# Layer-norm sums by additions of halves instead of strided reductions, and the last down-projection slab of two feed-forward blocks multiplied in three fp32r parts instead of whole in fp32

## The chip, the cores and the metric

One core of one Trainium2 chip runs the whole program. The metric is the device time of one execution in microseconds (us). Its engines are TensorE (PE, with its weight loads shown apart as PEld), VectorE (DVE), ScalarE (ACT), GpSimd (POOL) and SyncE (SP), which issues the transfers.

## The reference, cut to what matters

Two transformer-like blocks on 256 tokens of width 1024, everything in float32. The part at hand stands in the second block's convolution module and in the feed-forward network (FFN) beside it:

```
def layernorm(x, g, b):
    mu = mean(x, axis=-1)
    var = mean(square(x - mu), axis=-1)
    return (x - mu) * rsqrt(var + EPS) * g + b

def conformer_conv(h, ...):
    u = h @ w_pw1 + b_pw1
    a, g = split(u, 2)
    v = dwconv(a * sigmoid(g), w_dw, b_dw)      # 31 taps
    v = silu(layernorm(v, ln_g, ln_b))
    return v @ w_pw2 + b_pw2

def conv_ffn(h, w_up, w_dw, b_dw, w_down):      # hidden width 2816 = 22 tiles of 128
    u = dwconv(h @ w_up, w_dw, b_dw)            # 3 taps
    a, b = split(u, 2)
    return (silu(a) * b) @ w_down
```

The convolution module runs twice (on the context, then on the latent tokens). The FFN runs four times.

## The kernel before

**Slabs.** Activations lie transposed: 128 features per partition, 256 tokens in the free dimension, 8 tiles for the width 1024. All weights come in slabs of 128 x 2048 floats (1 MB) through a ring of three buffers (`raw`, `whi`, `wlo`). SP loads a slab into `raw`. A *split* slab is then cut in two fp32r parts: ACT writes the upper part (`hi`, L895, `whi`), DVE the rest (`lo`, L1396, `wlo`, columns 0 to 1983), and POOL the last 64 columns of the rest (L853). PE multiplies it by `mm3` (L2052 to L2054), three fp32r matmuls for each product: upper by upper, upper by the activation's lower part, lower by upper. A *whole* slab is not cut: PE takes `raw` in plain fp32 (L703). `kept_whole` says which is which, `DOWN_SPLIT` which down slabs of the FFNs `ffn0` and `ffn_ctx` are split.

**The FFN.** It has 11 steps j = 0 to 10 (`NJ` = 11), each with two up slabs and one down slab. I number the 33 slabs of one FFN from 0. Step 8 has the up slabs 23 and 24 and the down slab 28, step 9 has 26, 27 and 31, step 10 has 29, 30 and 32 (the last one, `use + "_end"`). Slabs 33 to 36 are those of the projection after the convolution (`pw2`). PE's order at the end is: up 26, 27, down 28, up 29, 30, down 31, down 32, then `pw2` slab 33, a mean over squares (`means`, L2153), 34, and so on. For each step ACT writes the first tap from PSUM (`tap`, L504), DVE adds the other taps (`taps`, L592, half 0 into `cva`, half 1 into `cvb`), ACT applies SiLU (L528), DVE multiplies (L617, this is the FFN's middle activation). For a split down slab ACT and DVE then also cut this activation in `m_hi` (L540) and `m_lo` (L626); for a whole one PE reads `cvb` as it is.

**The hosted convolution.** `ffn0` and `ffn_ctx` each carry the convolution module of one copy as "host" work: between the FFN's own instructions, at fixed (j, place) points, DVE and ACT do the 31 taps, and at the end the layer norm: at step 8 `ln_sum` (sum of the 8 tiles of `acc`), PE's `ln_mean`, `ln_centre` (L1579); at step 9 ACT's squares, `ln_fold` (sums of the squares), PE's `ln_var`, ACT's root, `ln_scale` (L1583, L1587); at step 10 ACT's `ln_silu` in two halves of four tiles (L979, with the copies L975 into `h_hi` or `g_hi`), DVE's `ln_lo` (L1592). PE's means multiply the partial sums by a matrix of 1/1024 (L2146), which adds over partitions. The output of this norm is what `pw2` multiplies.

**What sets the order.** Each engine runs its own written-out list; semaphores join them, and an instruction that waits holds everything behind it on its engine. On ACT the call of `hi` for slab 32 stands at the start of step 10, the ones for slabs 33 and 34 behind all of step 10; on DVE `lo` for slab 33 stands behind `ln_lo`. `hi` waits for the slab's transfer and for PE to be done with the slab that last used the same `whi` buffer (three slabs back). Behind the FFN, DVE adds the result to the residual (L1800 for `ffn0`, L1617 for `ffn_ctx`), ACT squares it, DVE folds the squares (L1404, L1406) and PE's `means` uses them behind slab 33.

Of the kernel before, what the change touches and what calls it, by code (L numbers as in the profile page):

```python
# [21 lines left out]
ALU = mybir.AluOpType  # L22
AX = mybir.AxisListType

P = 128
T = 256
# [13 lines left out]
NJ = D_FF // SLABC  # L40
FT = D_FF // P
TAPS = 3
CONV_TAPS = 31
DOWN_SPLIT = (NJ - 3, NJ - 2)
ADD_SLOTS = [(0, 1), (0, 2)] + [(1, at) for at in range(3)] + [(j, at) for j in range(2, NJ - 3) for at in range(3)]
OWN_SLOTS = [j for j in range(2, NJ - 3)]
PRODUCTS = len(ADD_SLOTS)
# [139 lines left out]
def kept_whole():  # L187

    out = []
    for use, i in KEYS:  # L190
        ffn = use.removesuffix("_end")
        if use == "lead":
            out.append(STREAM[i][0] == "ada")
        elif use.startswith("ada"):
            out.append(True)
        elif ffn in DOWN_WHOLE:
            out.append(use != ffn or (i >= 4 and i % 3 == 1 and (i - 4) // 3 not in DOWN_SPLIT))
        else:
            out.append(False)
    return out  # L200
# [75 lines left out]
def build(nc, io):  # L276
# [10 lines left out]
    with ctx:  # L287
# [7 lines left out]
        ps = ctx.enter_context(nc.psum_tensor("ps", [P, 8, 512], F32))  # L295
# [17 lines left out]
        bufA = sb("bufA", [P, SLAB])  # L313
# [8 lines left out]
        ones = sb("ones", [P, P])  # L322
# [12 lines left out]
        def flat(a):  # L335
            names = "abc"[:len(a.shape) - 1]
            return a.rearrange(f"p {' '.join(names)} -> p ({' '.join(names)})")
# [12 lines left out]
        acc = sra  # L350
# [7 lines left out]
        lstd = g_flat[:, late + 2 * T + 3 * P:late + 4 * T + 3 * P].rearrange("p (a t) -> p a t", a=2)  # L358
# [3 lines left out]
        ctx_sq, ctx_y = flat(mqk[:, :, :, :]), flat(sra[:, :, :])  # L362
# [40 lines left out]
        dve_order, act_order, pool_order = sem("dve_order"), sem("act_order"), sem("pool_order")  # L403
# [25 lines left out]
        sg_done, v_done, pads_done, dw_done = sem("sigmoid_done"), sem("glu_done"), sem("pads_cleared"), sem("dwconv_folded")  # L429
        mu_done, cen_done, lsq_done, var_done = sem("ln_mean_done"), sem("ln_centred"), sem("ln_squared"), sem("ln_var_done")  # L430
        lfold_done = sem("ln_folded")
# [955 lines left out]
        def _(dve):  # L1387
            order = Tally(dve_order)
# [174 lines left out]
            def ln_sum(q):  # L1563

                dve.wait_ge(prod_used, PRODUCTS * (q + 1))
                dve.wait_ge(dve_order, order.value())
                if q:
                    dve.wait_ge(lnorm_done, 2 * q)
                dve.tensor_reduce(lstd[:, 0, :], acc[:, :, :].rearrange("p t n -> p n t"), AX.X, ALU.add).then_inc(dw_done, 1)

            def ln_fold(q):
                for i in range(2):
                    dve.wait_ge(lsq_done, 2 * q + i + 1)
                    dve.tensor_reduce(lstd[:, i, :], ctx_sq[:, 1024 * i:1024 * i + 1024].rearrange("p (t n) -> p n t", n=T),  # L1574
                                      AX.X, ALU.add).then_inc(lfold_done, 1)

            def ln_centre(q):
                dve.wait_ge(mu_done, q + 1)
# [470 lines left out]
        def _(pe):  # L2049
# [92 lines left out]
            def mean(sums, bank, done, ready, first):  # L2142

                for i, s in enumerate(sums):
                    pe.wait_ge(ready, first + i + 1)
                    ins = pe.matmul(ps[:, bank, 0:T], ones[:, :], s, start=(i == 0), stop=(i == len(sums) - 1))  # L2146
                ins.then_inc(done, 1)
# [8 lines left out]
            def means_of_pairs(n, sq, k0, k1, bank=4):  # L2156
# [6 lines left out]
                if k1 == 4:  # L2163
                    ins.then_inc(ms_done, 1)

            def ln_mean(q):
                mean([lstd[:, 0, :]], 0, mu_done, dw_done, q)

            def ln_var(q):
                mean([lstd[:, 0, :], lstd[:, 1, :]], 1, var_done, lfold_done, 2 * q)  # L2170

            def conv_pe(q):

# [650 lines left out]
```

## Time and profile before

| what | us |
|---|---|
| median of 3 runs (lowest to highest) | 1391.59 (1390.79 to 1392.91) |
| the profiled execution's own time | 1392.44 |
| its span in the trace | 1390.7 |
| PE busy in the span | 1365.9 |
| DVE busy | 988.7 |
| ACT busy | 839.6 |
| POOL busy | 401.9 |

The trace covers the span of the profiled execution; 1.7 us of its time lie around it. Busy is the time in which at least one instruction of an engine runs; a matmul that waits for the one in front of it counts as busy. PE is busy almost throughout, so what matters is where PE stops, and how long its own instructions take.

### The profile page before, as it was taken

How to read it: one execution, taken by the hardware profiler on the slowest of the kernel's cores; microseconds unless marked ns; L12 is line 12 of the kernel's file. 1: busy time of each engine (PE TensorE's matmuls, PEld its weight loads, DVE VectorE, ACT ScalarE, POOL GpSimd, SP SyncE). 2: the span in 40 equal slices, each digit the busy share in tenths (PEclk: the TensorE clock that was granted, in tenths of full speed). 3: DMA queues.
4: the chain of work that ended last, by engine and by line, in shares of the span. 5: the costliest groups of instructions: out<-in, count | busy, mean ns of one | idle time of the engine just before them, and what ended most of it. 6: DMA issues, size and time to landing. Idle time of an engine off the chain costs nothing.

```text
span 1390.7 us, 26228 instructions
## 1 busy us (share of the span) xinstructions
PE 1365.9 (98%) x10670; PEld 1269.9 (91%) x10670; DVE 988.7 (71%) x1292; ACT 839.6 (60%) x1214; POOL 401.9 (29%) x194
## 2 busy tenths in 40 slices
PE   7999999999999999999999999999999999999997
PEld 4888889999999999999999999999998868999996
DVE  3322684868799998878999989766667696654446
ACT  3532555647888856567888575555544486644554
POOL 1452434233110011241100101656652201233332
PEclk9999999999999999999999999999999999999999
DMA  8776765455343454674434547655554713455551
GB/s 315 267 262 244 266 233 214 158 197 192 147 182 158 156 200 177 263 268 160 158 160 180 214 148 273 219 212 214 214 185 180 271 45 127 182 182 181 181 185 57
DMA packets 39576, 272.07 MB, mean 196 GB/s; under 512 B 4612, under 2 KB 5892, under 8 KB 6974
## 3 DMA queue, kind: packets, MB, share of 16 engines
q1 hardware_dynamic: 39486, 270.81, 52.7%
q8 instruction: 64, 1.05, 0.3%
q14 instruction: 26, 0.21, 0.0%
HBM read 269.73 MB, written 1.06 MB: 195 GB/s over the span
## 4 chain that ended last, share of the span: by engine, by line
PE 89%; DVE 7%; ACT 2%; DMA 1%; issue 1%; SPq 0%; DVEq 0%; ACTq 0%
PE ps L2052 23%; PE ps L2053 22%; PE ps L2054 22%; PE ps L703 9%; PE ps L2198 3%; PE ps L2089 2%; DVE wlo L1396 2%; DMA raw<-w_dram 1%; PE ps L2099 1%; PE ps L2566 1%; PE ps L2552 1%; DVE gates L1574 1%; ACT whi L895 1%; PE ps L2501 1%; PE ps L2248 1%
## 5 line engine op out<-in xcount | busy, mean ns | idle before, releaser
L853 POOL TENSOR_TENSOR wlo<-raw,whi 128x64 fp32r<-128x64 f32 (+1 forms) x185 | 399.6, 2162 | 968.5 <-ACT whi L895 968.3
L895 ACT ACTIVATE whi<-raw 128x2048 fp32r<-128x2048 f32 x185 | 352.8, 1911 | 358.9 <-PE ps L2054 223.1
L1396 DVE TENSOR_TENSOR wlo<-raw,whi 128x1984 fp32r<-128x1984 f32 (+1 forms) x185 | 338.7, 1832 | 309.2 <-ACT whi L895 309.2
L2052 PE MATMUL ps<-h_hi,whi 128*128 128x256 f32 x1232 | 354.1, 287 | 0.0
L2053 PE MATMUL ps<-h_lo,whi 128*128 128x256 f32 x1232 | 348.4, 283 | 0.0
L2054 PE MATMUL ps<-h_hi,wlo 128*128 128x256 f32 x1232 | 348.4, 283 | 0.0
L2052 PE MATMUL ps<-g_hi,whi 128*128 128x256 f32 x1040 | 298.4, 287 | 0.0
L2053 PE MATMUL ps<-g_lo,whi 128*128 128x256 f32 x1040 | 294.2, 283 | 0.0
L2054 PE MATMUL ps<-g_hi,wlo 128*128 128x256 f32 x1040 | 294.1, 283 | 0.0
L2052 PEld LDWEIGHTS ps<-h_hi,whi 128*128 128x128 f32 x1232 | 236.0, 192 | 8.0 <-issue 6.8
L2053 PEld LDWEIGHTS ps<-h_lo,whi 128*128 128x128 f32 x1232 | 236.1, 192 | 0.8
L2054 PEld LDWEIGHTS ps<-h_hi,wlo 128*128 128x128 f32 x1232 | 236.1, 192 | 0.0
L2052 PEld LDWEIGHTS ps<-g_hi,whi 128*128 128x128 f32 x1040 | 199.4, 192 | 3.7 <-issue 2.9
L2053 PEld LDWEIGHTS ps<-g_lo,whi 128*128 128x128 f32 x1040 | 199.4, 192 | 0.4
L2054 PEld LDWEIGHTS ps<-g_hi,wlo 128*128 128x128 f32 x1040 | 199.4, 192 | 0.0
L703 PE MATMUL ps<-cvb,raw 128*128 128x256 f32 x576 | 127.4, 379 | 0.5 <-DVE cvb L617 0.5
L703 PEld LDWEIGHTS ps<-cvb,raw 128*128 128x128 f32 x576 | 108.2, 190 | 14.9 <-issue 0.9
L995 ACT ACTIVATE bufA<-gates,cols 128x256 f32<-128x256 f32 x192 | 79.5, 502 | 23.4 <-DVE sra L1523 23.4
L592 DVE SCALAR_TENSOR_TENSOR cvb<-ps,cols,cvb 128x255 f32<-128x255 f32 (+1 forms) x176 | 76.5, 476 | 9.9 <-ACT cvb L504 6.6
L995 ACT ACTIVATE bufB<-gates,cols 128x256 f32<-128x256 f32 x176 | 72.8, 502 | 17.5 <-DVE sra L1523 17.5
L592 DVE SCALAR_TENSOR_TENSOR cva<-ps,cols,cva 128x255 f32<-128x255 f32 (+1 forms) x176 | 76.5, 475 | 3.3 <-DVE cva L592 0.3
L2052 PE MATMUL ps<-m_hi,whi 128*128 128x256 f32 x272 | 77.0, 283 | 0.0
(318 smaller groups left out, 1936.2 us busy)
## 6 DMA issues: line engine op xcount, KB each, us to landing
raw<-w_dram SPq DMA_DIRECT2D x243, 1024.0 KB, 4.9
sra<-w_dram SPq DMA_DIRECT2D x2, 1024.0 KB, 6.0
mqk<-w_dram SPq DMA_DIRECT2D x2, 1024.0 KB, 5.8
brev<-w_dram SPq DMA_DIRECT2D x2, 1024.0 KB, 7.6
gates<-w_dram SPq DMA_DIRECT2D x2, 1024.0 KB, 8.5
xlat<-xT_dram SPq DMA_DIRECT2D x2, 512.0 KB, 4.5
brev<-w_first_keys_dram SPq DMA_DIRECT2D x1, 1024.0 KB, 9.3
brev<-bias_rows SPq DMA_DIRECT2D x1, 1024.0 KB, 8.7
```

What stands on the lines that cost most here:

```text
L592: ins = dve.scalar_tensor_tensor(out, ps[:, 2 * par + half, m * T + src:m * T + src + n], w, out, ALU.mult, ALU.add)
L703: ins = pe.matmul(ps[:, 4 + m // 2, (m % 2) * T:(m % 2) * T + T], wf[:, k, m * P:m * P + P], cvb[:, par, k, :], start=(first and k == 0 an ...
L853: pool.tensor_tensor(wlo[:, g.slot, part], raw[:, g.slot, part], whi[:, g.slot, part].bitcast(F32), ALU.subtract).then_inc(lo2_done, 1)
L895: act.activation(whi[:, g.slot, :], raw[:, g.slot, :], ACT.Copy).then_inc(hi_done, 1)
L995: ins = act.activation(buf[:, t * T:t * T + T], vpad[:, t, k:k + T], ACT.Copy, scale=col("dw_w", KT * k + t))
L1396: dve.tensor_tensor(wlo[:, g.slot, part], raw[:, g.slot, part], whi[:, g.slot, part].bitcast(F32), ALU.subtract)\
L1574: dve.tensor_reduce(lstd[:, i, :], ctx_sq[:, 1024 * i:1024 * i + 1024].rearrange("p (t n) -> p n t", n=T), AX.X, ALU.add).then_inc(lfold_d ...
L2052: pe.matmul(out, w[0], x[0], start=start, stop=False, skip_group_check=True)
L2053: pe.matmul(out, w[0], x[1], start=False, stop=False, skip_group_check=True)
L2054: return pe.matmul(out, w[1], x[0], start=False, stop=stop, skip_group_check=True)
L2089: pe.matmul(ps[:, bank, m * T:m * T + T], w[i][:, k, m * P:m * P + P], x[0][:, k, :], start=(k == 0 and m == 0 and i == 0), stop=False, sk ...
L2198: ins = pe.matmul(ps[r:r + QUAD, bank, 0:SLABC], cnd[:, c:c + QUAD], w[:, t, :], start=(t < 4 and k == 0), stop=(t >= 4 and k == n - 1), s ...
```

## The change

It does three things. `ln_sum` and `ln_fold` no longer use a reduction over strided elements, but add halves in place: 8 tiles to 4 to 2 (into `bufA`) for the sum, and 4 to 2 twice and then 2 + 2 for the squares. The last addition over the remaining two tiles is left to PE, in `total`, which waits once and multiplies two tiles: `ln_mean` has two matmuls where it had one, `ln_var` two as before. The wait of the second `ln_sum` on the norm before it is gone. And `DOWN_SPLIT` has step 10 too, so that slab 32 of `ffn0` and of `ffn_ctx` is split, with its `m_hi` and `m_lo`.

```
-DOWN_SPLIT = (NJ - 3, NJ - 2)
+DOWN_SPLIT = (NJ - 3, NJ - 2, NJ - 1)
...
-            out.append(use != ffn or (i >= 4 and i % 3 == 1 and (i - 4) // 3 not in DOWN_SPLIT))
+            out.append(NJ - 1 not in DOWN_SPLIT if use != ffn else i >= 4 and i % 3 == 1 and (i - 4) // 3 not in DOWN_SPLIT)
...
                 dve.wait_ge(prod_used, PRODUCTS * (q + 1))
                 dve.wait_ge(dve_order, order.value())
-                if q:
-                    dve.wait_ge(lnorm_done, 2 * q)
-                dve.tensor_reduce(lstd[:, 0, :], acc[:, :, :].rearrange("p t n -> p n t"), AX.X, ALU.add).then_inc(dw_done, 1)
+                order.mark(dve.tensor_tensor(bufA[:, 0:4 * T], flat(acc[:, 0:4, :]), flat(acc[:, 4:8, :]), ALU.add))
+                dve.wait_ge(dve_order, order.value())
+                dve.tensor_tensor(bufA[:, 0:2 * T], bufA[:, 0:2 * T], bufA[:, 2 * T:4 * T], ALU.add).then_inc(dw_done, 1)

             def ln_fold(q):
                 for i in range(2):
                     dve.wait_ge(lsq_done, 2 * q + i + 1)
-                    dve.tensor_reduce(lstd[:, i, :], ctx_sq[:, 1024 * i:1024 * i + 1024].rearrange("p (t n) -> p n t", n=T),
-                                      AX.X, ALU.add).then_inc(lfold_done, 1)
+                    half = ctx_sq[:, 1024 * i:1024 * i + 512]
+                    order.mark(dve.tensor_tensor(half, half, ctx_sq[:, 1024 * i + 512:1024 * i + 1024], ALU.add))
+                dve.wait_ge(dve_order, order.value())
+                dve.tensor_tensor(ctx_sq[:, 0:512], ctx_sq[:, 0:512], ctx_sq[:, 1024:1536], ALU.add).then_inc(lfold_done, 1)
...
+            def total(rows, bank, done, ready, n):
+
+                pe.wait_ge(ready, n + 1)
+                for i, row in enumerate(rows):
+                    ins = pe.matmul(ps[:, bank, 0:T], ones[:, :], row, start=(i == 0), stop=(i == len(rows) - 1))
+                ins.then_inc(done, 1)
+
             def ln_mean(q):
-                mean([lstd[:, 0, :]], 0, mu_done, dw_done, q)
+                total([bufA[:, T * i:T * i + T] for i in range(2)], 0, mu_done, dw_done, q)

             def ln_var(q):
-                mean([lstd[:, 0, :], lstd[:, 1, :]], 1, var_done, lfold_done, 2 * q)
+                total([ctx_sq[:, T * i:T * i + T] for i in range(2)], 1, var_done, lfold_done, q)
```

On VectorE, in step 10 of `ffn0`, this stood before (the middle line L1587 is `ln_scale`, L592 the taps, L617 the middle activation, L1592 `ln_lo`, L1396 the `lo` of slab 33):

```order
L1587 TENSOR_TENSOR sra<-sra,gates 128x1024
L592 SCALAR_TENSOR_TENSOR cva<-ps,cols,cva 128x254 [waits tap0_done]
L592 SCALAR_TENSOR_TENSOR cva<-ps,cols,cva 128x254
L592 SCALAR_TENSOR_TENSOR cva<-ps,cols,cva 128x255 [waits dve_order]
L592 SCALAR_TENSOR_TENSOR cva<-ps,cols,cva 128x255
L592 SCALAR_TENSOR_TENSOR cvb<-ps,cols,cvb 128x254 [waits tap0_done]
L592 SCALAR_TENSOR_TENSOR cvb<-ps,cols,cvb 128x254
L592 SCALAR_TENSOR_TENSOR cvb<-ps,cols,cvb 128x255 [waits dve_order]
L592 SCALAR_TENSOR_TENSOR cvb<-ps,cols,cvb 128x255
L617 TENSOR_TENSOR cvb<-cva,cvb 128x512 [waits conv_done,silu_done]
L1592 TENSOR_TENSOR h_lo<-mqk,h_hi 128x512 [waits conv_act_hi_done] x4
L1396 TENSOR_TENSOR wlo<-raw,whi 128x1984 [waits slab_hi_done]
```

In the changed kernel the same place on VectorE begins and ends like this (line numbers behind the edits are 2 higher, so L1589 is the old L1587 and L1594 the old L1592):

```order
L1589 TENSOR_TENSOR sra<-sra,gates 128x1024
L1396 TENSOR_TENSOR wlo<-raw,whi 128x1984 [waits slab_hi_done]
L592 SCALAR_TENSOR_TENSOR cva<-ps,cols,cva 128x254 [waits tap0_done]
...
L617 TENSOR_TENSOR cvb<-cva,cvb 128x512 [waits conv_done,silu_done]
L626 TENSOR_TENSOR m_lo<-cvb,m_hi 128x512 [waits host_mid_hi_done]
L1594 TENSOR_TENSOR h_lo<-mqk,h_hi 128x512 [waits conv_act_hi_done] x4
L1396 TENSOR_TENSOR wlo<-raw,whi 128x1984 [waits slab_hi_done]
```

So `lo` of slab 32 now stands ahead of the taps of step 10, and `m_lo` ahead of `ln_lo`.

On ScalarE, at the end of step 10 of `ffn0`, this stood before (L528 is the SiLU of step 10, L979 and L975 are the second half of `ln_silu`, L895 the `hi` of slabs 33 and 34):

```order
L528 ACTIVATE cva<-cva 128x512 [waits conv_done]
L979 ACTIVATE mqk<-sra,cols 128x256 [waits ln_normed] x2
L975 ACTIVATE h_hi<-mqk 128x512 [waits ln_silu_done]
L979 ACTIVATE mqk<-sra,cols 128x256 [waits ln_normed] x2
L975 ACTIVATE h_hi<-mqk 128x512 [waits ln_silu_done] x2
L895 ACTIVATE whi<-raw 128x2048 [waits slab_used,slab_landed1]
L895 ACTIVATE whi<-raw 128x2048 [waits slab_used,slab_landed2]
```

In the changed kernel ScalarE has there:

```order
L528 ACTIVATE cva<-cva 128x512 [waits conv_done]
L540 ACTIVATE m_hi<-cvb 128x512 [waits slab_used,mid_done]
L979 ACTIVATE mqk<-sra,cols 128x256 [waits ln_normed] x2
L975 ACTIVATE h_hi<-mqk 128x512 [waits ln_silu_done]
L979 ACTIVATE mqk<-sra,cols 128x256 [waits ln_normed] x2
L975 ACTIVATE h_hi<-mqk 128x512 [waits ln_silu_done] x2
L895 ACTIVATE whi<-raw 128x2048 [waits slab_used,slab_landed1]
L895 ACTIVATE whi<-raw 128x2048 [waits slab_used,slab_landed2]
```

The added `m_hi` waits for the middle activation of step 10 (`mid_done`), and the second half of `ln_silu` and both `hi` stand behind it. A further `hi`, that of slab 32, now stands at the start of step 10.

## Rows read from the trace of the kernel before

**Rows 1.** Page: busy time (share) of TensorE; chain that ended last, by engine.

```profile
PE 1365.9 (98%) x10670; PEld 1269.9 (91%) x10670; DVE 988.7 (71%) x1292; ACT 839.6 (60%) x1214; POOL 401.9 (29%) x194
PE 89%; DVE 7%; ACT 2%; DMA 1%; issue 1%; SPq 0%; DVEq 0%; ACTq 0%
```

**Rows 2.** Windows, TensorE: stretch, its length, PE busy, clock, DMA share, GB/s.

```profile
493.02:499.93 6.91, 6.91 (x35) 1.00 0.01 2
499.93:505.68 5.75, 5.75 (x50) 1.00 0.78 293
536.33:543.48 7.15, 7.15 (x34) 1.00 0.00 0
```

**Rows 3.** Timeline of TensorE (start, us, instruction [idle before]): the means.

```profile
505.68 0.59 PE L2146 MATMUL ps<-gates,ones 128*128 128x256 f32 x2
...
506.22 0.28 PE L2053 MATMUL ps<-g_lo,whi 128*128 128x256 f32 x1
...
549.06 1.02 PE L2153 MATMUL ps<-bufB,ones 128*128 128x256 f32 x4
```

**Rows 4.** Waits, 500 to 552: waiter, releaser, us, times, longest.

```profile
PEld ps L703 <- issue: 0.4, 1, 0.4
PEld ps L2146 <- DVE gates L1574: 0.3, 1, 0.3
```

**Rows 5.** Timeline of VectorE, 500 to 552, end of `ffn0`.

```profile
500.31 3.84 DVE L1569 TENSOR_REDUCE gates<-sra 128x256 f32<-128x2048 f32 x1
...
506.91 2.23 DVE L1396 TENSOR_TENSOR wlo<-raw,whi 128x1984 fp32r<-128x1984 f32 x1 [0.28 <-ACT whi L895]
509.05 0.81 DVE L626 TENSOR_TENSOR m_lo<-cvb,m_hi 128x512 fp32r<-128x512 f32 x1
...
514.12 3.93 DVE L1574 TENSOR_REDUCE gates<-mqk 128x256 f32<-128x1024 f32 x2
...
524.28 2.22 DVE L1396 TENSOR_TENSOR wlo<-raw,whi 128x1984 fp32r<-128x1984 f32 x1
...
528.80 2.36 DVE L1587 TENSOR_TENSOR sra<-sra,gates 128x1024 f32<-128x1024 f32 x2
531.08 1.77 DVE L592 SCALAR_TENSOR_TENSOR cva<-ps,cols,cva 128x254 f32<-128x254 f32 x4
533.60 1.78 DVE L592 SCALAR_TENSOR_TENSOR cvb<-ps,cols,cvb 128x254 f32<-128x254 f32 x4 [0.75 <-ACT cvb L504]
535.49 0.69 DVE L617 TENSOR_TENSOR cvb<-cva,cvb 128x512 f32<-128x512 f32 x1
...
539.45 2.23 DVE L1396 TENSOR_TENSOR wlo<-raw,whi 128x1984 fp32r<-128x1984 f32 x1 [0.86 <-ACT whi L895]
...
546.25 1.29 DVE L1404 TENSOR_TENSOR bufB<-bufB 128x512 f32<-128x512 f32 x2
547.57 0.69 DVE L1406 TENSOR_TENSOR bufB<-bufB 128x512 f32<-128x512 f32 x1
```

**Rows 6.** Timeline of ScalarE, the same stretch.

```profile
504.96 1.92 ACT L895 ACTIVATE whi<-raw 128x2048 fp32r<-128x2048 f32 x1 [6.04 <-DMA raw<-w_dram]
...
521.17 1.90 ACT L895 ACTIVATE whi<-raw 128x2048 fp32r<-128x2048 f32 x1
524.40 0.64 ACT L540 ACTIVATE m_hi<-cvb 128x512 fp32r<-128x512 f32 x1 [1.32 <-DVE cvb L617]
...
533.99 1.08 ACT L979 ACTIVATE mqk<-sra,cols 128x256 f32<-128x256 f32 x2
...
537.52 3.70 ACT L895 ACTIVATE whi<-raw 128x2048 fp32r<-128x2048 f32 x2
```

**Rows 7.** Timeline of GpSimd: its share of a slab.

```profile
550.19 2.37 POOL L853 TENSOR_TENSOR wlo<-raw,whi 128x64 fp32r<-128x64 f32 x1 [8.05 <-ACT whi L895]
```

**Rows 8.** Timeline of VectorE behind `ffn_ctx`, the second copy.

```profile
823.27 2.22 DVE L1396 TENSOR_TENSOR wlo<-raw,whi 128x1984 fp32r<-128x1984 f32 x1 [0.86 <-ACT whi L895]
...
832.00 0.69 DVE L1406 TENSOR_TENSOR bufB<-bufB 128x512 f32<-128x512 f32 x1
```

## The prediction

> **What bounds the kernel now.** I read the page first: TensorE is busy 98% of the span and the chain that ended last runs through it for 89% [rows 1]. So only two things move the time: a shorter or longer list of TensorE's own instructions, and stops of TensorE. Next the waits of the stretch in which the change lies (500 to 552 us for `ffn0`, the same picture 823.27 - 539.45 = 283.8 us later for `ffn_ctx` [rows 5, 8]): TensorE stops twice, 0.3 us before `ln_var`'s second matmul, which waits for the reduction L1574, and 0.4 us before the whole slab 32 (L703), whose middle activation (L617, 535.49 + 0.69 = 536.18) is just late [rows 4, 5]. The reader should see from this that TensorE comes to slab 32 at 535.9, and that VectorE and ScalarE are only just in time there: behind 514 VectorE has almost no idle time in its rows [rows 5]. What is added to these two engines there is not hidden.
>
> **What TensorE's own list gains.** In a dense stretch a whole down slab (32 records) takes 6.91 us, a slab of 48 fp32r matmuls 5.75 [rows 2], so splitting slab 32 saves 1.16 us. From its start to the next slab it took 7.15 [rows 2], 0.24 more than dense; in the new form I take 5.75 + 0.1 = 5.85. `ln_mean` gets a second fp32 matmul. One costs 0.42: behind it the second fp32r matmul starts at 506.22, where without it it would start at 505.68 + 0.12 (the pitch, 5.75 / 48) [rows 2, 3]. The 0.3 us wait in `ln_var` goes, but part of it lay over the matmuls' own time, so I count 0.15 of it. Net TensorE reaches slab 32 at 535.9 - 0.15 + 0.42, so 0.3 later, at 536.15.
>
> **What the additions of halves gain on VectorE.** `ln_sum` falls from 3.84 to one addition of 1024 elements (2.36 / 2 = 1.18, L1587) and one of 512 (0.69): 1.9 saved [rows 5]. `ln_fold` falls from 3.93 to 1.29 + 0.69 (L1404 and L1406 do just this): again 1.9 saved [rows 5]. But where does the time go?
> - The first 1.9 go nowhere. Soon behind `ln_sum` VectorE waits for ScalarE's `hi` of slab 28 (the 0.28 idle before 506.91), and that starts at 504.96 because of its transfer [rows 5, 6]. The wait becomes 2.2 us and everything behind it stands as before. TensorE did not wait for `ln_sum` either.
> - Of the second 1.9, half arrives. The `lo` of slab 31 (524.28) could start at 522.4, but its `hi` runs from 521.17 to 523.07 [rows 5, 6], and that, behind the root and the SiLU, hangs on `ln_var`, which comes about 0.2 later. So 523.35: 0.95 saved. `ln_scale` ends at 530.15 and not 531.08.
>
> **What the split of slab 32 costs.** Step by step in `ffn0`:
> - VectorE's `lo` of slab 32 stands ahead of the taps. 524.28 + 2.22 overlaps its follower by 0.1, so 2.13 [rows 5]. Taps of half 0 start at 530.15 + 2.15 = 532.3 instead of 531.08. Half 1 before waited 0.75 for ScalarE (533.60); that cover takes up part: it starts at 534.05, 0.45 later. The middle activation is written at 536.6, not 536.18 [rows 5].
> - ScalarE's `m_hi` waits for it and takes 0.64 [rows 6], VectorE's `m_lo` 0.81 [rows 5]: slab 32 may start at 536.6 + 0.65 + 0.8 + two hand-overs of 0.06 = 538.15. TensorE, there at 536.15, waits 2.0 us, and ends at 538.15 + 5.85 = 544.0. Before it was 543.48. So the split's own saving is already more than gone: +0.5.
> - Behind `m_hi` on ScalarE are queued the second half of `ln_silu` and then the `hi` of slab 33. Before, they started right behind the SiLU, at 533.99 and 537.52 [rows 6]: 3.53 us for the half. Now the half starts at 537.2, so `hi` of slab 33 at 540.75, and VectorE's `lo` at 542.7, not 539.45 [rows 5]: +3.25. GpSimd's 64 columns of the same slab take 2.37 beside it [rows 7], against VectorE's 2.2, and TensorE needs both. So `pw2` starts at 542.7 + 2.4 + 0.05 = 545.15. Before it was 543.48, and TensorE waits another 1.15: +1.7.
> - VectorE next adds the residual, cuts slab 34 and folds the squares. From `lo` of slab 33 to the end of L1406 that is 547.57 + 0.69 - 539.45 = 8.81 us [rows 5], so the fold is ready at 551.5. TensorE is through slab 33 at 545.15 + 5.75 = 550.9 and waits 0.7. Its `means` start at 551.6, before at 549.06 [rows 3]: +2.5. That margin was under 1 us, so it is what is late next. Behind it the same chains hang on TensorE's own progress and shift with it; I give nothing back.
>
> `ffn_ctx` is the same but for its residual: 832.00 + 0.69 - 823.27 = 9.42 from `lo` to fold [rows 8], 0.6 longer, and so +3.1. Sum: 2.5 + 3.1 = **+5.6 us**. The `lo` of slab 32 also lets SP load slab 35 some 11 us earlier than TensorE's end of slab 32 did; nothing on TensorE waited for it, so I count zero, and if another load were late it would be a gain, not a loss.
>
> The trace is of an execution of 1392.44, with a span of 1390.7; it is 0.85 above the median of 1391.59. The sum is a difference of the span, so I put it on the median: 1391.6 + 5.5, **1397.1 us**.
>
> **A rule weighed.** The row gives 3.84 us for the reduction of 2048 elements and 1.9 for the two additions in its place [rows 5]. The Trainium skill ("VectorE: DVE Perf Modes", Rules for kernel authors) says that `tensor_reduce` is the slowest VectorE operation and that one on a hot path is worth restructuring. The rows agree on the price, but not that this path is hot: by the rule 7.6 us of VectorE's time in the two copies would come off the end, by the rows at most 0.95 in each reaches slab 32, and without the split the additions alone would be worth 0.1 to 0.3 us a copy.
>
> **Bounds of what the trace doesn't show.** `total` with its one wait: zero to 0.4 a copy. A split slab 32 behind a wait: 5.75 to 6.1. `m_hi` plus `m_lo` with the hand-overs: 1.4 (the nearest rows without hand-over) to 1.9. Residual and fold under a busy GpSimd: plus 0 to 0.4. Together -1.0 to +2.0 on the sum for both copies.
>
> **The rivals.**
> 1. *All of VectorE's saving arrives* (no change, chance 0.08). Then slab 32's parts are ready 2.8 earlier, at 535.35; TensorE does not wait and ends at 542.0, but `m_hi` still pushes the `hi` of slab 33: its `lo` starts at 539.9, `pw2` at 542.35 (-1.1), the fold is ready at 548.75 (-0.3), in `ffn_ctx` +0.3. Sum about 0: 1391.6. Against it: the transfer behind the 6.04 us idle on ScalarE [rows 6].
> 2. *Only TensorE's list counts* (faster, 0.05). The order behind `m_hi` costs nothing, slab 32 starts at 536.15 and ends at 542.0, and slab 33's `lo` and the fold are ready in time: -1.45 a copy, -2.9: 1388.7. It decides itself where `lo` of slab 33 ends by 542 and the fold by 547.8; before they ended at 541.7 and 548.26 [rows 5], so it needs that ScalarE's queue is not moved at all. The list says that it is.
> 3. *Slab 32 waits, but nothing behind it does* (no change, 0.06): +0.5 a copy, 1392.6. It needs `lo` of slab 33 by 543.8, while I have 544.9.
> 4. *A further stop behind `means`* (slower, 0.06). The next fold, for `means` before `pw2` slab 36, is also just in time; if TensorE waits there 1 us a copy more, 1399 to 1401.
> My forecast as worked out has 0.75.
>
> **How the numbers follow.** A difference of 0.2% (2.8 us) is about what a measurement of this kernel can tell from none. The forecast's own range is 1396 to 1399. For 8 in 10 the range takes in rival 3 and the near half of rival 4: 1392.6 to 1399.6; rivals 1 and 2 stay outside. Slower by over 0.2%: the forecast and rival 4, 0.81; within: rivals 1 and 3, 0.14; faster 0.05.
>
> **What the new profile would show.** Right if: VectorE's idle before the `lo` of slab 28 is 2.2 us; TensorE waits for `m_lo` some 2 us before slab 32, then about 1 us for L1396 or L853 before `pw2`, then 0.7 to 1.3 us before `means`; `hi` of slab 33 starts 3.2 us later against slab 32's activation. Wrong if: the `lo` of slab 31 follows without ScalarE's `hi` (rival 1), or if `pw2` follows slab 32 without a gap (rivals 2 and 3), or if the copies differ by much more than 0.6 us.

## The result and the profile after

The changed kernel takes 1398.61 us (median of 5 runs, 1395.18 to 1401.67), the kernel before in the same session 1390.79 (5 runs, 1389.42 to 1392.91). The ratio is 1.0053 with a 95% interval of 1.0038 to 1.0068: by this ratio it is slower by 7.4 us, interval 5.3 to 9.5 (the two medians differ by 7.8). A second session, with the changed kernel unchanged (told below), gave 1.0032 (1.0017 to 1.0048), or 4.4 us (medians 5.2 apart). The two intervals overlap. The prediction was +5.6 and 1397.1, in the range of 1392.6 to 1399.6.

The page of the changed kernel, busy time and the chain that ended last, beside [rows 1]:

```profile
span 1399.7 us, 26320 instructions
...
PE 1366.3 (98%) x10706; PEld 1271.8 (91%) x10706; DVE 983.5 (70%) x1300; ACT 843.7 (60%) x1218; POOL 407.9 (29%) x196
...
PE 88%; DVE 6%; ACT 2%; DMA 2%; issue 1%; SPq 0%; POOL 0%; DVEq 0%; ACTq 0%
```

VectorE has 5.2 us less work, TensorE 0.4 more, and the span is 9.0 longer. So the time is in stops of TensorE. Its weight loads show them (PEld: start, duration, what is loaded, idle before). Those with an idle time, in `ffn0` and then in `ffn_ctx`:

```profile
540.80 0.19 PEld L2054 LDWEIGHTS ps<-m_hi,whi 128*128 128x128 f32 x1 [2.07 <-issue]
547.96 0.19 PEld L2054 LDWEIGHTS ps<-h_hi,whi 128*128 128x128 f32 x1 [1.34 <-issue]
554.07 0.73 PEld L2155 LDWEIGHTS ps<-bufB,ones 128*128 128x128 f32 x4 [0.30 <-DVE bufB L1406]
...
827.11 0.19 PEld L2054 LDWEIGHTS ps<-m_hi,whi 128*128 128x128 f32 x1 [2.07 <-issue]
834.27 0.19 PEld L2054 LDWEIGHTS ps<-g_hi,whi 128*128 128x128 f32 x1 [1.34 <-issue]
841.12 0.73 PEld L2155 LDWEIGHTS ps<-bufB,ones 128*128 128x128 f32 x4 [1.05 <-DVE bufB L1406]
```

These are the stops before slab 32, before `pw2` slab 33 and before `means`, where before there were only 0.3 in `ln_var` and 0.4 ahead of slab 32 [rows 4]. The waits of TensorE's instructions from 500 to 560 name who is late:

```profile
PE ps L2054 <- DVE m_lo L626: 1.9, 1, 1.9
...
PE ps L2054 <- POOL wlo L853: 1.2, 1, 1.2
...
PEld ps L2155 <- DVE bufB L1406: 0.3, 1, 0.3
```

VectorE in the same stretch, beside [rows 5]. This execution came to the stretch 2.61 later than that of before (first weight load of slab 25 at 495.52 and at 492.91), so 2.61 is to be taken off a start before it is compared:

```profile
502.97 1.22 DVE L1567 TENSOR_TENSOR bufA<-sra 128x1024 f32<-128x1024 f32 x1
504.22 0.69 DVE L1569 TENSOR_TENSOR bufA<-bufA 128x512 f32<-128x512 f32 x1
...
509.55 2.23 DVE L1396 TENSOR_TENSOR wlo<-raw,whi 128x1984 fp32r<-128x1984 f32 x1 [2.14 <-ACT whi L895]
...
525.97 2.23 DVE L1396 TENSOR_TENSOR wlo<-raw,whi 128x1984 fp32r<-128x1984 f32 x1 [0.89 <-ACT whi L895]
...
530.62 2.36 DVE L1589 TENSOR_TENSOR sra<-sra,gates 128x1024 f32<-128x1024 f32 x2
532.90 2.22 DVE L1396 TENSOR_TENSOR wlo<-raw,whi 128x1984 fp32r<-128x1984 f32 x1
...
538.61 0.69 DVE L617 TENSOR_TENSOR cvb<-cva,cvb 128x512 f32<-128x512 f32 x1
540.00 0.69 DVE L626 TENSOR_TENSOR m_lo<-cvb,m_hi 128x512 fp32r<-128x512 f32 x1 [0.69 <-ACT m_hi L540]
...
545.33 2.22 DVE L1396 TENSOR_TENSOR wlo<-raw,whi 128x1984 fp32r<-128x1984 f32 x1 [1.03 <-ACT whi L895]
...
553.32 0.69 DVE L1406 TENSOR_TENSOR bufB<-bufB 128x512 f32<-128x512 f32 x1
```

The additions save what they should. All that `ln_sum` saves turns into idle time before the `lo` of slab 28 (2.14, before 0.28). Of what `ln_fold` saves about half does, before the `lo` of slab 31 (0.89, before none), and the other half arrives: that `lo` starts at 525.97 - 2.61 = 523.36, before at 524.28 [rows 5]. ScalarE shows the queue behind `m_hi`, beside [rows 6]:

```profile
539.33 0.63 ACT L540 ACTIVATE m_hi<-cvb 128x512 fp32r<-128x512 f32 x1 [1.85 <-DVE cvb L617]
539.87 1.08 ACT L979 ACTIVATE mqk<-sra,cols 128x256 f32<-128x256 f32 x2
...
543.40 3.70 ACT L895 ACTIVATE whi<-raw 128x2048 fp32r<-128x2048 f32 x2
```

The `hi` of slab 33 starts at 543.40 - 2.61 = 540.79, before at 537.52 [rows 6]: 3.27 later.

To compare kernels without what lies outside, I use **the stretch**: from the first weight load of slab 25 to the weight load of the `means` behind `pw2` slab 33. Before it is 548.95 - 492.91 = 56.04 in `ffn0` and 56.07 in `ffn_ctx`; after, 554.07 - 495.52 = 58.55 and 841.12 - 781.82 = 59.30. So +2.51 and +3.23, together +5.74. The span differs by 9.0. The rest is 2.61 ahead of the stretch, where no code of the change has run yet, and 0.65 behind the second copy. The 2.61 are not the change's: the same changed kernel in the second session came to the stretch at 491.48, which is 4.04 earlier and also ahead of the kernel before.

### The profile page after: what moved, and what is told of

Its sections match the earlier page's. It is cut to its first block, busy times and chain, and to the rows that moved or that the text cites. A ratio compares the mean times of both kernels' runs of the same rounds, so it can differ in the third digit from the quotient of the medians.

```text
span 1399.7 us, 26320 instructions
## 1 busy us (share of the span) xinstructions
PE 1366.3 (98%) x10706; PEld 1271.8 (91%) x10706; DVE 983.5 (70%) x1300; ACT 843.7 (60%) x1218; POOL 407.9 (29%) x196
## 3 DMA queue, kind: packets, MB, share of 16 engines
q8 instruction: 64, 1.05, 0.3%
## 4 chain that ended last, share of the span: by engine, by line
PE 88%; DVE 6%; ACT 2%; DMA 2%; issue 1%; SPq 0%; POOL 0%; DVEq 0%; ACTq 0%
PE ps L2054 23%; PE ps L2055 22%; PE ps L2056 22%; PE ps L703 8%; PE ps L2207 3%; PE ps L2091 2%; DMA raw<-w_dram 2%; DVE wlo L1396 2%; PE ps L2101 1%; PE ps L2575 1%; ACT whi L895 1%; PE ps L2561 1%; PE ps L2510 1%; PE ps L2257 1%; DVE tiny L1902 0%
## 5 line engine op out<-in xcount | busy, mean ns | idle before, releaser
L853 POOL TENSOR_TENSOR wlo<-raw,whi 128x64 fp32r<-128x64 f32 (+1 forms) x187 | 405.7, 2171 | 971.5 <-ACT whi L895 971.2
L895 ACT ACTIVATE whi<-raw 128x2048 fp32r<-128x2048 f32 x187 | 356.5, 1910 | 361.7 <-PE ps L2056 228.5
L1396 DVE TENSOR_TENSOR wlo<-raw,whi 128x1984 fp32r<-128x1984 f32 (+1 forms) x187 | 339.3, 1816 | 320.5 <-ACT whi L895 320.4
L703 PE MATMUL ps<-cvb,raw 128*128 128x256 f32 x512 | 113.2, 379 | 0.0
L703 PEld LDWEIGHTS ps<-cvb,raw 128*128 128x128 f32 x512 | 96.2, 190 | 12.4
L2054 PE MATMUL ps<-m_hi,whi 128*128 128x256 f32 x304 | 86.2, 283 | 3.8 <-DVE m_lo L626 3.8
L2055 PE MATMUL ps<-m_lo,whi 128*128 128x256 f32 x304 | 86.0, 283 | 0.0
L2056 PE MATMUL ps<-m_hi,wlo 128*128 128x256 f32 x304 | 86.0, 283 | 0.0
```

The source lines that it names most:

```text
L703: ins = pe.matmul(ps[:, 4 + m // 2, (m % 2) * T:(m % 2) * T + T], wf[:, k, m * P:m * P + P], cvb[:, par, k, :], start=(first and k == 0 an ...
L853: pool.tensor_tensor(wlo[:, g.slot, part], raw[:, g.slot, part], whi[:, g.slot, part].bitcast(F32), ALU.subtract).then_inc(lo2_done, 1)
L895: act.activation(whi[:, g.slot, :], raw[:, g.slot, :], ACT.Copy).then_inc(hi_done, 1)
L1396: dve.tensor_tensor(wlo[:, g.slot, part], raw[:, g.slot, part], whi[:, g.slot, part].bitcast(F32), ALU.subtract)\
L2054: pe.matmul(out, w[0], x[0], start=start, stop=False, skip_group_check=True)
L2055: pe.matmul(out, w[0], x[1], start=False, stop=False, skip_group_check=True)
```

## The experiments

The stretch of each run (copy 1, copy 2), TensorE's stop before slab 32 in it, and the measured time. Where there is one run, no ratio is given; there the stretch and the stops are the evidence. Each ratio is to runs of the kernel before in the same session; its medians there were 1390.79, then 1390.00, 1390.20 and 1390.22.

| kernel | stretch | stop before slab 32 | median us (runs) | ratio to before, 95% |
|---|---|---|---|---|
| before | 56.04, 56.07 | 0.43 | | |
| after | 58.55, 59.30 | 2.07 | 1398.61 (5) | 1.0053, 1.0038 to 1.0068 |
| after, repeated | 58.56, 59.31 | 2.07 | 1395.36 (10) | 1.0032, 1.0017 to 1.0048 |
| additions only | 55.80, 55.80 | none | 1388.79 (11) | 0.9988, 0.998 to 0.9997 |
| split only | 59.44, 60.12 | 3.10 | 1398.62 (6) | 1.0056, 1.0042 to 1.007 |
| `hi` of slab 33 early | 58.27, 56.97 | 2.06 | 1393.28 (9) | 1.0024, 1.0014 to 1.0034 |
| GpSimd, slabs 31 and 32 | 59.05, 59.81 | 2.57 | 1396.49 (1) | |
| GpSimd, slab 32 | 58.70, 59.44 | 2.22 | 1398.88 (1) | |
| all three moves | 58.67, 58.79 | 2.71 | 1395.70 (10) | 1.0044, 1.0028 to 1.006 |
| two moves, no GpSimd | 56.27, 56.46 | 1.56 | 1389.95 (12) | 1.0002, 0.9988 to 1.0015 |
| additions, one matmul | 54.94, 54.95 | none | 1387.51 (12) | 0.9977, 0.9964 to 0.999 |
| `ln_sum` only | 56.03, 55.93 | 0.42 | 1392.99 (1) | |
| `ln_fold` only | 54.94, 54.94 | none | 1386.34 (1) | |

The load of `ln_mean` stands 12.65 behind the first load of slab 25 in every kernel (to 0.01), so the stretch can be counted from either.

**The change taken apart.** My theory: the loss is all the split's, through the two queues (VectorE ahead of the middle activation, ScalarE behind `m_hi`), and the additions gain a little. The rival: the additions or the second matmul cost something too. First the additions alone, so the changed kernel with

```
-DOWN_SPLIT = (NJ - 3, NJ - 2, NJ - 1)
+DOWN_SPLIT = (NJ - 3, NJ - 2)
```

> The additions of halves and `total` without the split of slab 32. The stretch is that from TensorE's first weight load of slab 25 to that of the `means` behind `pw2` slab 33: 56.04 us (first copy) and 56.07 (second) before, 58.55 and 59.30 after the change. Queue theory (the split's work on VectorE and ScalarE costs the time): 55.9 in both copies, since slab 32 is whole again and ready before TensorE comes to it (its wait of 0.4 goes), while `ln_mean` has a matmul of 0.42 more and `ln_var` loses its 0.3 wait; whole kernel -0.3 us, ratio 0.998 to 1.001. VectorE's idle before the `lo` of slab 28 is still 2.1 us. Rival (the additions themselves or the changed waits cost the time): the stretch stays at 57.5 or more.

Measured: a stretch of 55.80 in both copies, where before it was 56.04, and 0.9988. TensorE stops nowhere in it. The additions cost nothing; they gain 0.24 in the first copy and 0.27 in the second. The rival falls as a reason for the loss; the second matmul does cost its 0.43, as the kernel with one matmul shows below.

Then the split alone: the kernel before with its strided reductions, and only `DOWN_SPLIT` and the rule in `kept_whole` as in the change.

> The split of slab 32 with the old strided reductions. Queue theory: VectorE comes to the `lo` of slab 32 some 0.95 us later than in the changed kernel, so TensorE waits 3.2 us before slab 32, 1.2 before `pw2`, 0.7 and 1.3 before `means`: the stretch is 59.4 and 60.0 us, the whole kernel +7.3 us, ratio 1.004 to 1.007. Rival (VectorE's lateness isn't what holds slab 32, but ScalarE's `hi` of slab 32 is): the stretch is that of the changed kernel, 58.55 and 59.30.

Measured: 59.44 and 60.12. TensorE's weight loads with an idle time, in this kernel:

```profile
537.75 0.19 PEld L2052 LDWEIGHTS ps<-m_hi,whi 128*128 128x128 f32 x1 [3.10 <-issue]
551.02 0.73 PEld L2153 LDWEIGHTS ps<-bufB,ones 128*128 128x128 f32 x4 [0.20 <-DVE bufB L1406]
```

The stop before slab 32 is 3.10 and not 2.07. Counted from the start of the stretch, slab 32 starts at 46.17 here and at 45.28 in the changed kernel: these 0.89 are what reaches it of the additions in `ln_fold`. The expected stop of 1.2 before `pw2` is gone, because slab 32 itself took 7.23 here and not 5.82, at a lower TensorE clock (below). So the split alone costs 3.40 and 4.05 in the copies, and the additions give 0.9 and 0.8 of it back.

**The queue behind `m_hi`.** If the stops before `pw2` and `means` come from what is queued behind `m_hi`, they go when the `hi` of slab 33 is issued ahead of it. In the changed kernel, ScalarE and then VectorE:

```
                 tap(1, j, par)
+                if ends and whole:
+                    hi(g + (RING + 1))
...
-            for k in range(ahead):
+            for k in range(1 if whole else 0, ahead):
                 hi(g + (RING + 1 + k))
...
                        .then_inc(hostmid_lo, host_step(j))
+                    if ends:
+                        lo(g + (RING + 1))
...
-            lo(g + (RING + 1))
+            if not whole:
+                lo(g + (RING + 1))
```

> The changed kernel with only two calls moved: ScalarE's `hi` of slab 33 stands behind the tap of half 1 of step 10, where ScalarE idles 1.5 us, and VectorE's `lo` of slab 33 right behind `m_lo` of step 10. Queue theory: the 2 us wait before slab 32 stays (2.0 to 2.5), the waits before `pw2` (1.3) and `means` (0.3 and 1.05) go; the stretch is 56.7 and 57.0 us, the whole kernel +1.5 us against before, ratio 1.000 to 1.003. Rival (the waits before `pw2` come from slab 32's late end itself, not from the order behind `m_hi`): the stretch stays above 58.

Measured: one stop in each copy, before slab 32, 2.06 and 2.07; none before `pw2` or `means`. Copy 2 has 56.97, as expected, copy 1 58.27. The windows of this kernel say why (length, PE busy and number of instructions, PEld, DVE, ACT, POOL, then the granted clock, DMA share and GB/s):

```profile
536.60:540.00 3.40, 3.40 (x18) 3.40 (x17) 3.40 (x6) 3.40 (x5) 0.00 (x0) 0.50 0.38 99
...
822.60:826.00 3.40, 3.40 (x30) 3.40 (x30) 3.40 (x6) 3.40 (x5) 0.00 (x0) 1.00 0.43 92
```

In copy 1 the granted clock was 0.50 (1.2 GHz and not 2.4) for 3.4 us in the middle of slab 32: 18 matmuls recorded where copy 2 has 30. That is what sets the copies apart: slab 32 took 7.23 in copy 1 and 5.74 in copy 2. The queue is confirmed as the cause of the two later stops: 59.30 - 56.97 = 2.3 us in copy 2. The two calls were moved together, so which of the two queues holds more of it is not shown.

**GpSimd takes half of the rest.** To shorten VectorE's queue ahead of the middle activation I gave GpSimd 1024 of the 2048 columns of `lo` in place of 64, for slabs 31 and 32:

```
+    if use in DOWN_WHOLE and i == 3 * NJ - 2 or use in ("ffn0_end", "ffn_ctx_end"):
+        return 1024
```

> The changed kernel with GpSimd taking 1024 of the 2048 columns of slabs 31 and 32 instead of 64, so that VectorE's two `lo` take 1.36 and not 2.22 us each. Queue theory (VectorE's work ahead of slab 32 sets its start): everything behind comes 1.7 us earlier, TensorE waits 0.4 before slab 32 and not 2.0; the stretch is 56.9 and 57.6 us. Rival (ScalarE's `m_hi` or GpSimd is what is late): the wait before slab 32 stays at 1.5 or more, since GpSimd's 3.4 us for 1024 columns end later than VectorE's.

Measured: the stop before slab 32 is 2.57, longer than without. A miss. GpSimd and VectorE of this kernel show it:

```profile
519.94 6.26 POOL L855 TENSOR_TENSOR wlo<-raw,whi 128x1024 fp32r<-128x1024 f32 x2 [7.10 <-ACT whi L897]
```

```profile
519.90 1.23 DVE L1398 TENSOR_TENSOR wlo<-raw,whi 128x1024 fp32r<-128x1024 f32 x1 [0.93 <-ACT whi L897]
521.04 2.90 DVE L628 TENSOR_TENSOR m_lo<-cvb,m_hi 128x512 fp32r<-128x512 f32 x1
523.87 1.74 DVE L1587 RECIPROCAL gates<-gates 128x256 f32<-128x256 f32 x1
525.64 2.78 DVE L1591 TENSOR_TENSOR sra<-sra,gates 128x1024 f32<-128x1024 f32 x2
528.35 1.21 DVE L1398 TENSOR_TENSOR wlo<-raw,whi 128x1024 fp32r<-128x1024 f32 x1
529.49 1.77 DVE L594 SCALAR_TENSOR_TENSOR cva<-ps,cols,cva 128x254 f32<-128x254 f32 x4
```

The `lo` itself fell from 2.22 to 1.2, but `m_lo` took 2.90 where it took 0.81, and the two multiplications of `ln_scale` 2.78 where they took 2.36. That is 2.5 lost for 2.0 saved, and the stop grew by 0.5. The first of GpSimd's two instructions ends at 523.40, while `m_lo`, begun at 521.04, ends at 523.94. To see whether slab 31's share was the trouble, the same for slab 32 alone:

```
+    if use in ("ffn0_end", "ffn_ctx_end"):
+        return 1024
```

> The changed kernel with GpSimd taking 1024 columns of slab 32 alone, no longer of slab 31. Contention theory (in e4_pool_share VectorE's `m_lo` of step 9 and the `ln_scale` took 2.9 and 2.8 us beside GpSimd's 1024 columns of slab 31, instead of 0.8 and 2.4, which ate the saving): here GpSimd's run lies beside the taps; if these read their second input from PSUM they are not slowed, TensorE waits 1.1 us before slab 32 and not 2.07, and the stretch is 57.6 and 58.3. Rival (any VectorE work beside a long GpSimd run is slowed): the wait is 2 us or more, and the taps of step 10 take over 2 us and not 1.77.

Measured: 2.22, a miss again. GpSimd and VectorE:

```profile
525.87 2.40 POOL L855 TENSOR_TENSOR wlo<-raw,whi 128x1024 fp32r<-128x1024 f32 x1 [1.14 <-ACT whi L897]
```

```profile
526.98 3.51 DVE L1591 TENSOR_TENSOR sra<-sra,gates 128x1024 f32<-128x1024 f32 x2
530.42 1.21 DVE L1398 TENSOR_TENSOR wlo<-raw,whi 128x1024 fp32r<-128x1024 f32 x1
531.55 1.77 DVE L594 SCALAR_TENSOR_TENSOR cva<-ps,cols,cva 128x254 f32<-128x254 f32 x4
```

Now `ln_scale` runs 3.51: 1.15 more than its 2.36. GpSimd's instruction ends at 525.87 + 2.40 = 528.27, 1.29 behind `ln_scale`'s start. So the first multiplication seems to stand until GpSimd is through, and what `lo` saves (1.0) is paid just ahead of it. The Trainium skill says this ("SBUF — State Buffer", SBUF: two separate sides, and Who interferes with whom): GpSimd and a VectorE instruction with two SBUF inputs share one pair of ports, whoever starts first holds it for the whole instruction, and with at most one SBUF input, outside its two-port modes, VectorE is free of it. The rows agree in size: 528.27 plus two multiplications of 1.18 is 530.63, and `ln_scale` ended at 530.49. They agree in kind too: L1587, the reciprocal, has one SBUF input, ran beside GpSimd in the kernel with both shares (at 523.87) and took its usual 1.74.

**All moves together.** The early `hi` of slab 33, GpSimd's 1024 columns of slab 32, and the second half of `ln_scale` moved behind the middle activation of step 10:

```
                 if hosting:
                     beside(1)
+                if whole and ends:
+                    beside(1.5)
...
+                    if (j, at) == (NJ - 1, 1.5):
+                        ln_scale_half(KT // 2)
```

> The changed kernel with three moves: `hi` and `lo` of slab 33 early as in e3_hi33_early, GpSimd with 1024 columns of slab 32, and the second half of `ln_scale` (1.2 us) behind the middle activation of step 10, where VectorE waits 0.7 for `m_hi`. Queue theory: slab 32's parts are ready 1.0 + 0.6 us earlier than in the changed kernel, TensorE waits 0.4 to 0.6 before it and nowhere behind it: the stretch is 55.2 to 55.6 in both copies, whole kernel -1 us against before, ratio 0.998 to 1.001. Rival (three-part matmuls of slab 32 bring nothing whatever the order): the stretch is not below before's 56.0.

Measured: 58.67 and 58.79, where 55.2 to 55.6 was expected, with a stop of 2.71 and a lower clock in slab 32 in both copies (it took 6.99 and 7.11). The two halves of `ln_scale` in this kernel:

```profile
524.81 2.37 DVE L1602 TENSOR_TENSOR sra<-sra,gates 128x1024 f32<-128x1024 f32 x1
...
533.69 1.22 DVE L1602 TENSOR_TENSOR sra<-sra,gates 128x1024 f32<-128x1024 f32 x1
```

The same instruction takes 2.37 beside GpSimd (its row reads 523.70 to 526.11) and 1.22 without it. Two causes were left for the miss: GpSimd's share, or that the early `hi` and the late half get in each other's way. So the same kernel without the share (the two lines of `pool_words` taken out again):

> e7_all_moved without the GpSimd share: `hi` and `lo` of slab 33 early, and the second half of `ln_scale` behind the middle activation of step 10; GpSimd takes 64 columns of slab 32 again. Displacement theory (in e6_pool_slab32 and e7_all_moved the first multiplication of `ln_scale` ran behind or beside GpSimd's 2.4 us and was later by as much as VectorE's shorter `lo` gave back): without GpSimd's long run the parts of slab 32 are ready 0.6 us earlier than in e3_hi33_early, TensorE waits 1.4 to 1.6 us before it, the stretch is 56.3 to 56.5 us where its clock holds and 57.7 to 57.9 where it reads 0.50 behind the stop; ratio 1.000 to 1.003. Rival (the late half of `ln_scale` or the early `hi` of slab 33 made e7_all_moved late): the wait is 2.5 us or more again.

Measured: 56.27 and 56.46, as the first theory said, and 1.0002. TensorE and VectorE of this kernel:

```profile
532.12 0.19 PEld L2065 LDWEIGHTS ps<-m_hi,whi 128*128 128x128 f32 x1 [1.56 <-issue]
```

```profile
522.46 1.23 DVE L1600 TENSOR_TENSOR sra<-sra,gates 128x1024 f32<-128x1024 f32 x1
523.60 2.22 DVE L1403 TENSOR_TENSOR wlo<-raw,whi 128x1984 fp32r<-128x1984 f32 x1
```

Taking GpSimd's share away brings the stop from 2.71 to 1.56, and no other stop is left. It is GpSimd that made the miss. The way is not VectorE's own queue, where the shorter `lo` makes up for all but 0.15 of the 1.14 that the multiplication loses. It goes through ScalarE, first in the kernel with the share and then in the one without (which comes to the stretch 2.35 earlier):

```profile
527.22 2.08 ACT L988 ACTIVATE mqk<-sra,cols 128x256 f32<-128x256 f32 x4 [2.69 <-DVE sra L1602]
533.08 0.69 DVE L621 TENSOR_TENSOR cvb<-cva,cvb 128x512 f32<-128x512 f32 x1 [0.53 <-ACT cva L532]
```

```profile
523.72 2.08 ACT L986 ACTIVATE mqk<-sra,cols 128x256 f32<-128x256 f32 x4 [1.54 <-DVE sra L1600]
529.58 0.69 DVE L619 TENSOR_TENSOR cvb<-cva,cvb 128x512 f32<-128x512 f32 x1 [0.38 <-ACT cva L530]
```

`ln_silu` waits for that first multiplication. Behind it ScalarE runs without a gap through the tap of half 1, the early `hi` of slab 33 and the SiLU, for which the middle activation waits in both kernels. So all of it, `ln_silu` and the middle activation and the stop, is 1.15 later. The stretch differs by more, 2.40 and 2.33; the rest is the clock, since slab 32 takes 5.74 in this kernel.

With the queues on both sides eased the split is about even with the kernel before: the stop of 1.56 is still more than the 1.16 that it saves on the slab, and the additions without the split are ahead of it (55.80 against 56.27 and 56.46).

**The changed kernel again**, without an edit, beside the others of its session.

> The changed kernel unaltered, on the chip of the others. Queue theory: the stretch is again 58.6 and 59.3, so +5.7 us; whole kernel +5 to +8, ratio 1.004 to 1.006. Clock theory (behind a stop of 2 to 3 us TensorE's granted clock read 0.50 for some 3.4 us, in both copies of e2_split_only and one copy of e3_hi33_early, in none of the changed kernel's profile): if it falls here too in a copy, that copy's slab 32 takes 7.2 us and not 5.85, and the wait before `pw2` is shorter by as much, so that the stretch hardly grows. Rival: no such fall, and the spread of the times lies elsewhere.

Measured: the stretch is 58.56 and 59.31, the same to 0.01, and the time 1395.36. So the stretch repeats, and what differs between the two profiled executions lies outside it, most of it ahead of it (495.52 against 491.48 at its start).

**What the additions are worth, and which.** The additions only, with a third one of 256 elements on VectorE, so that `ln_mean` and `ln_var` have one matmul each:

```
-                dve.tensor_tensor(bufA[:, 0:2 * T], bufA[:, 0:2 * T], bufA[:, 2 * T:4 * T], ALU.add).then_inc(dw_done, 1)
+                order.mark(dve.tensor_tensor(bufA[:, 0:2 * T], bufA[:, 0:2 * T], bufA[:, 2 * T:4 * T], ALU.add))
+                dve.wait_ge(dve_order, order.value())
+                dve.tensor_tensor(bufA[:, 0:T], bufA[:, 0:T], bufA[:, T:2 * T], ALU.add).then_inc(dw_done, 1)
...
-                total([bufA[:, T * i:T * i + T] for i in range(2)], 0, mu_done, dw_done, q)
+                total([bufA[:, 0:T]], 0, mu_done, dw_done, q)
```

and the same for the squares.

> The additions of halves without the split, and with a third addition on VectorE (256 elements, some 0.4 us) in `ln_sum` and in `ln_fold`, so that `ln_mean` and `ln_var` have one matmul each. VectorE idles 2.1 and 0.9 us behind these places in e1_adds_only. Queue theory: TensorE's list is 0.42 shorter at each of the two places; slab 32's activation is ready 0.6 us before TensorE comes to it in e1_adds_only, so of 0.84 some 0.6 arrive: the stretch is 55.0 to 55.2 us in both copies (55.8 in e1_adds_only), the whole kernel -1.9 us against before, ratio 0.997 to 1.000. Rival (VectorE's added work there is not free): the stretch is 55.8 or more.

Measured: 54.94 and 54.95, and 0.9977: faster than before by 3.2 us (1.4 to 5.0). It beats both kernels. Against the additions of the change it gains 0.86 a copy, two fp32 matmuls of 0.43 each, where only 0.6 was expected to arrive; the third addition takes 0.43 on VectorE, which has room for it there.

Then each half of it alone on the kernel before. First `ln_sum` by three additions with its one matmul:

> The kernel before with `ln_sum` alone as three additions of halves (`ln_mean` keeps one matmul). Queue theory: VectorE's 1.5 us are lost in its wait for the `hi` of slab 28; the stretch is 56.04 and 56.07 as before. Rival (VectorE's time counts wherever it is saved): 55.6 or less.

Measured: 56.03 and 55.93, so nothing within 0.14. VectorE of this kernel waits where the reduction stood before:

```profile
507.66 2.23 DVE L1396 TENSOR_TENSOR wlo<-raw,whi 128x1984 fp32r<-128x1984 f32 x1 [1.61 <-ACT whi L895]
```

Then `ln_fold` by three rounds, with one matmul in `ln_var` and the reduction in `ln_sum` left:

> The kernel before with `ln_fold` alone as three rounds of additions and one matmul in `ln_var`. Queue theory: the 0.3 wait and one matmul of 0.42 go from `ln_var` and the 0.4 wait before slab 32 goes: the stretch is 54.95 in both copies, all of what e5_one_matmul gained. Rival (both sums share the gain): about 55.5.

Measured: 54.94 in both copies, the same as both together. So all of the gain is `ln_fold`'s: VectorE saves about as much in `ln_sum`, but ahead of a wait for a transfer. The 1.10 of `ln_fold` are about the stops of 0.30 in `ln_var` and 0.43 before slab 32 and one fp32 matmul less (0.43).

## Why the prediction was right, step by step

Direction, mechanism and range held. Each step beside what the profile after shows for `ffn0`, starts less 2.61:

| step | predicted | shown |
|---|---|---|
| idle before `lo` of slab 28 | 2.2 | 2.14 |
| `lo` of slab 31 starts, 0.95 earlier | 523.35 | 523.36, 0.92 earlier |
| second matmul of `ln_mean` | 0.42 | 0.43 |
| TensorE reaches slab 32 later by | 0.3 | 0.25 |
| slab 32: waits, starts | 2.0, 538.15 | 2.07, 538.19 |
| slab 32 ends | 544.0 | 544.01 |
| `hi` of slab 33 starts | 540.75 | 540.79 |
| wait before `pw2`, its start | 1.15, 545.15 | 1.34, 545.35 |
| wait before `means` | 0.7 | 0.30 |
| the same in `ffn_ctx` | 1.3 | 1.05 |
| the two copies | +2.5, +3.1 | +2.51, +3.23 |

- **The chain to slab 32** held to 0.1. It was a chain of rows from this very stretch, each with its follower.
- **The wait before `pw2` was 0.2 too small, the one before `means` 0.4 too large.** For `pw2` I took 0.05 from the end of GpSimd's part to the start of TensorE; it is about 0.2. For the fold I counted 8.81 from the `lo` of slab 33, and it took 553.32 + 0.69 - 545.33 = 8.68. The two errors have opposite signs, and a later start of `pw2` is by itself a shorter wait behind it.
- **The whole.** The sum was +5.6, the two stretches +5.74. The medians gave +7.8 in one session and +5.2 in the other. Part of the first is not the change's: in its profiled execution 2.61 us were lost ahead of the stretch, all of them by 249 us (the granted clock is 0.93 in the window 50 to 100, in the execution of before 1.00), and the repeated kernel did not lose them (491.48, granted clock 1.00 there). Over all the traces the stretch begins anywhere from 487.35 to 493.69, and at 495.52 in this one. The changed kernel's executions spread over 6.5 us. So the mechanism is right by the stretches. That the median of 1398.61 lies in the range, 1.0 below its upper end, is partly luck; the range held no term for what varies ahead of the stretch. (The last line of the sum adds 5.5 where the sum is 5.6, a slip of 0.1.)
- **The rule that was weighed** would have made the additions alone worth 7.6 us. They measured 1.7 us (0.4 to 2.8) faster. The trace's answer stands: a reduction that is slow is worth restructuring only if something waits for it. `ln_sum` in front of a transfer gave 0, `ln_fold` gave what TensorE waited for, and a matmul less where the third addition was made on VectorE.
- **The rivals.** Rival 1 falls by the idle times of 2.14 and 0.89; rival 2 by the stop of 2.07 before slab 32; rivals 2 and 3 by the stops of 1.34 before `pw2`; rival 4 because behind `means` there is only the 0.41 that the kernel before has there too.
- **What I left out** is the granted clock. In the changed kernel it held at 1.00 in slab 32 in the one trace and fell in copy 2 of the other, where slab 32 took 7.23, outside the bound of 5.75 to 6.1. It did not show in the sum, because the wait before `pw2` took it up.

## What to carry to other kernels

Where one engine is busy 98% of the time, an edit is worth what happens at its stops: list for each stop who arrives last, and what the edit puts ahead of that one and behind it on its own queue. A saving ahead of a wait for something else is worth nothing, and a conversion that makes the bound engine's work 1.16 us shorter is a loss if it lengthens the chain that this engine waits for by 2. Sizes worked out from rows of the same stretch held to 0.25 us here but for one of 0.4 (`means`). The experiments that missed assumed that a neighbouring engine costs nothing (GpSimd's larger share) or that the clock holds (copy 1 with the `hi` of slab 33 early).

## What the runs showed of the hardware

**TensorE's clock behind a short stop.** Seven traces have a stop of 2.06 to 3.10 us before slab 32, in two copies each. In 8 of these 14 the granted clock fell to about half at the end of the stop or shortly behind it: split only in both copies (windows of 3.4 us with 0.54 and 0.51), `hi` of slab 33 early in copy 1 (0.50), GpSimd for slab 32 in both, all moves in both (there already in the stop's last 0.6 us in copy 1: 0.76 from 534.50 to 535.60), and the changed kernel repeated in copy 2. It held in the other six, among them both copies of the changed kernel's first trace at 2.07 and of GpSimd for slabs 31 and 32 at 2.57. In this part of the program it never fell where the stop was 1.56 or less. So the length of the stop alone does not decide it, and what does stays open. Where it fell, slab 32 took 6.99 to 7.23 us, where it held 5.74 to 5.82: 1.2 to 1.5 longer. Where another wait stood behind (before `pw2`), it swallowed that and the stretch was the same: copy 2 of the repeated kernel has 59.31 with the fall, the first trace 59.30 without. Where nothing stood behind, it cost all of it: from the first load of slab 32 to that of `means` are 12.99 in copy 1 with the `hi` of slab 33 early, and 11.50 in copy 1 of the kernel with two moves, where the clock held: 1.49. (Copy 2 of the former has 11.69, of which 0.19 is a wait before `means` of its own.)

**GpSimd and VectorE side by side.** In these traces a VectorE instruction with two SBUF inputs is not slowed by GpSimd in proportion, it stands until GpSimd's instruction ends: 0.81 became 2.90, 1.22 became 2.37. The other way round too: GpSimd's 64 columns take 0.32 us where nothing holds them, and 2.37 where they start beside VectorE's 2.2 us of `lo`, which was in the rows of before already [rows 7].
